# Up products of three feed-forward blocks read shifted activations, their second tile a copy

## What is computed

```
def conv_ffn(h, w_in, dw, w_out):          # layers 0 and 1
    u = causal_dwconv(h @ w_in, dw)        # [512,1024] @ [1024,5632]
    gate, val = u[..., :D_FF], u[..., D_FF:]
    return (jax.nn.silu(gate) * val) @ w_out    # [512,2816] @ [2816,1024]
...
    x = x + conv_ffn(rmsnorm(x, norm_ffn_g[layer]), ffn_w_in[layer], ffn_dw[layer], ffn_w_out[layer])
...
    a, val = jnp.split(rmsnorm_2(x, norm_ffn_g) @ w_up, 2, axis=-1)     # layer 2
    a = causal_dwconv_2(a, conv_w, conv_b)
    return x + (jax.nn.gelu(a) * val) @ w_down
```

## Time and profile before

| | us |
|---|---|
| median of 3 runs | 2596.2 (2595.59 to 2596.39) |
| the profiled execution, its own time | 2603.86 |
| its span | 2602.1 |
| TensorE busy in it | 2510.2 (96%) |
| DVE, ACT, POOL busy | 1336.2, 1123.0, 995.2 |
| mean granted clock | 0.985 |

### The profile page before, as it was taken

One profiled execution on the slowest core, in us unless ns is written; L12 is line 12 of the kernel. 1 busy time (PEld: TensorE's weight loads), 2 busy tenths in 40 slices (PEclk: granted clock), 3 DMA queues, 4 the chain that ended last, 5 costly groups with the idle time before them and its releaser, 6 DMA issues.

```text
span 2602.1 us, 62231 instructions
## 1 busy us (share of the span) xinstructions
PE 2510.2 (96%) x25266; PEld 2370.8 (91%) x25266; DVE 1336.2 (51%) x2034; ACT 1123.0 (43%) x1653; POOL 995.2 (38%) x488
## 2 busy tenths in 40 slices
PE   7999898999999999998999999999999999999998
PEld 6888886997999999977989999999998769999998
DVE  7666564513477741798523677622153344455521
ACT  8844445544433432425534344433245444444422
POOL 3333220562344444325423444444443104444442
PEclk9899999999999999999999999999999999999999
DMA  4221001351223233323222332233222103223232
GB/s 153 76 67 50 1 1 63 99 177 41 90 97 97 97 98 107 121 65 113 82 65 65 97 97 91 96 106 120 83 95 68 47 1 97 97 89 97 96 99 74
DMA packets 62180, 219.43 MB, mean 84 GB/s; under 512 B 6752, under 2 KB 9184, under 8 KB 61408
## 3 DMA queue, kind: packets, MB, share of 16 engines
q1 hardware_dynamic: 58880, 207.76, 24.8%
q10 hardware_dynamic: 3168, 9.75, 1.0%
HBM read 213.29 MB, written 4.19 MB: 84 GB/s over the span
## 4 chain that ended last, share of the span: by engine, by line
PE 83%; DVE 8%; issue 6%; ACT 2%; POOL 1%; DMA 0%; DVEq 0%; POOLq 0%; ACTq 0%
PE psum L571 70%; DVE psum L2698 5%; PE psum L713 3%; PE psum L721 2%; PE psum L1072 1%; PE psum L1021 1%; PE psum L1251 1%; PE psum L1290 1%; POOL wl L520 1%; DVE psum L2269 1%; ACT wh L1382 0%; PE psum L1253 0%; PE psum L683 0%; PE psum L1060 0%; PE psum L1278 0%
## 5 line engine op out<-in xcount | busy, mean ns | idle before, releaser
L520 POOL TENSOR_TENSOR wl<-raw,wh 128x1024 fp32r<-128x1024 f32 x388 | 949.1, 2455 | 1461.8 <-ACT wh L1382 1461.7
L571 PE MATMUL psum<-acth,wh 128*128 128x256 f32 x3792 | 763.4, 283 | 18.3 <-DVE actl L2789 8.0
L571 PE MATMUL psum<-actl,wh 128*128 128x256 f32 x3792 | 752.8, 280 | 0.0
L571 PE MATMUL psum<-acth,wl 128*128 128x256 f32 x3792 | 752.4, 280 | 0.0
L1382 ACT ACTIVATE wh<-raw 128x1024 fp32r<-128x1024 f32 x388 | 407.1, 1056 | 624.0 <-PE psum L571 600.5
L571 PEld LDWEIGHTS psum<-acth,wh 128*128 128x128 f32 x3792 | 582.4, 189 | 35.8 <-issue 28.1
L571 PEld LDWEIGHTS psum<-actl,wh 128*128 128x128 f32 x3792 | 581.6, 189 | 0.0
L571 PEld LDWEIGHTS psum<-acth,wl 128*128 128x128 f32 x3792 | 581.1, 189 | 0.0
L2628 DVE TENSOR_TENSOR cu<-psum,rstd 128x512 f32<-128x512 f32 x132 | 91.0, 690 | 237.8 <-PE psum L571 220.6
L571 PE MATMUL psum<-hidh,wh 128*128 128x256 f32 x1056 | 209.5, 276 | 0.0
L571 PE MATMUL psum<-hidl,wh 128*128 128x256 f32 x1056 | 209.3, 276 | 0.0
(11 more groups left out here) (443 smaller groups left out, 4056.0 us busy)
## 6 DMA issues: line engine op xcount, KB each, us to landing
raw<-in_weights SPq DMA_DIRECT2D x388, 512.0 KB, 3.4
xt<-in_x SPq DMA_DIRECT2D x4, 512.0 KB, 5.5
xt<-in_x ACTq DMA_DIRECT2D x1, 2048.0 KB, 9.3
out_x<-xt SPq DMA_DIRECT2D x6, 256.0 KB, 2.3
mem<-in_mem ACTq DMA_DIRECT2D x1, 1024.0 KB, 11.1
memn<-memh ACTq DMA_DIRECT2D x1, 1024.0 KB, 5.6
memn<-meml ACTq DMA_DIRECT2D x1, 1024.0 KB, 9.1
memh<-memn ACTq DMA_DIRECT2D x1, 1024.0 KB, 4.7
```

The costliest lines, as they stand in the source:

```text
L520: pool.tensor_tensor(wl[:, s, :], raw[:, s, :], wh[:, s, :].bitcast(F32), ALU.subtract).then_inc(split_done, 1)
L571: ins = pe.matmul(out[:, n:n + HALF], w, m[:, n:n + HALF], start=first and n == 0, stop=last and n + HALF >= out.shape[1])
```

## The change

The activations of the three up stages go to new tensors `uph` and `upl`, 160 bytes above acth and actl and over the same memory, so at 192. The second tile of each up stage (tile 1) reads `firsth` and `firstl` instead, at zone + 49,184 and 16,384 above that, which is 224 beyond a multiple of 512. They are filled during `xo0`, `xo1` and `out2`: for each block ACT copies uph to firsth after its square, and DVE copies upl to firstl after its addition to rstd. Two semaphores count the copies, and tile 1 waits for 8 of each. Tile 1 is taken out of the loop, which now begins with tile 2; two tiles follow it instead of three. To make room, 256 bytes are added behind actl, `eps` moves into the tail of `par`, and `omu` moves to the end of the memory; `tmp`, `sq`, `rstd` and `zone` stay where they were. The other stages that read acth and actl are as before.

```diff
         acth = place("acth", [P, KT, T], F32R)
         actl = place("actl", [P, KT, T], F32R)
-        par = place("par", [P, NPAR])
+        cursor[0] += 256
+        uph, upl = (at("up" + n, [P, KT, T], F32R, act_at + 160 + 16384 * j) for j, n in enumerate("hl"))
+        par = place("par", [P, NPAR + 6])
+        eps = par[:, NPAR:NPAR + 6]
         common = place("common", [P, 3 * P])
-        omu = place("omu", [P, 7 * KT])
-        eps = place("eps", [P, 6])
+        omu = at("omu", [P, 7 * KT], F32, 229120)
...
         cu = place("cu", [P, 4, T + 2])
+        firsth, firstl = (at("first" + n, [P, KT, T], F32R, zone + 49184 + 16384 * j) for j, n in enumerate("hl"))
...
             def ffn(l):
                 up, norm = f"up{l}", f"norm_ffn{l}"
-                tile(up, 0, norm, acth, actl)
+                tile(up, 0, norm, uph, upl)
                 norm_total(norm)
-                dense(up, norm, acth, actl, units=2 * FT - 4, skip=1)
-                for j in range(2 * FT - 3, 2 * FT):
-                    tile(up, j, norm, acth, actl)
+                pe.wait_ge(first_hi, KT * (l + 1))
+                pe.wait_ge(first_lo, KT * (l + 1))
+                tile(up, 1, norm, firsth, firstl)
+                dense(up, norm, uph, upl, units=2 * FT - 4, skip=2)
+                for j in range(2 * FT - 2, 2 * FT):
+                    tile(up, j, norm, uph, upl)
...
+                        if again:
+                            act.wait_ge(hi_ready, i * 4 + (g0 + s + 1))
+                            hold()
+                            act.activation(again[:, i * 4 + s, :], h[:, i * 4 + s, :].bitcast(F32),
+                                           ACT.Identity).then_inc(first_hi, 1)
...
-                deltas_normed(f"xo{l}", 1, f"norm_ffn{l}")
+                deltas_normed(f"xo{l}", 1, f"norm_ffn{l}", h=uph, again=firsth)
...
+                        if again:
+                            dve.wait_ge(lo_ready, i * 4 + (g0 + s + 1 + SC))
+                            dve.tensor_copy(again[:, k, :], l[:, k, :].bitcast(F32)).then_inc(first_lo, 1)
```

More of the change, by code:

```diff
@@ L344, in build_program @@
         cu = place("cu", [P, 4, T + 2])
+        firsth, firstl = (at("first" + n, [P, KT, T], F32R, zone + 49184 + 16384 * j) for j, n in enumerate("hl"))
+        assert act_at % 512 == 32 and zone % 512 == 192
         cg, cv, sg = (place("ffn_" + n, [P, 2, T]) for n in ("cg", "cv", "sg"))
@@ L375, in build_program @@
         fmax, fneg, fsum, frec = (place("fox_" + n, [P, 8, 4]) for n in ("max", "neg", "sum", "rec"))
-        assert cursor[0] <= nc.sbuf_usable_end
+        assert cursor[0] <= 229120
         over = zone + 8192
@@ L428, in build_program @@
         mid_split = sem("mid_split")
+        first_hi, first_lo = sem("first_hi"), sem("first_lo")
         x_ready = sem("x_ready")
@@ L501, in _ @@
             sp.dma_start(common[:, :], dram["c_common"]).then_inc(common_in, 16)
-            sp.dma_start(par[:, :], dram["par"]).then_inc(par_in, 16)
+            sp.dma_start(par[:, 0:NPAR], dram["par"]).then_inc(par_in, 16)
             with sp.Fori(0, UNITS // SLOTS) as i:
@@ L1462, in deltas, with deltas_normed @@
                         weight_high(UNIT0[stage] + skip + s + SLOTS, i)
-            def deltas_normed(stage, per, norm, gain=None, h=acth):
+            def deltas_normed(stage, per, norm, gain=None, h=acth, again=None):
                 x0, sq0 = plan(stage, "x"), plan(norm, "sq")
@@ L2130, in hybrid @@
                         sigmoids(2 * k + 6, 2 * k + 8)
-                deltas_normed("out2", 1, "norm_ffn2")
+                deltas_normed("out2", 1, "norm_ffn2", h=uph, again=firsth)
             def last_norm():
@@ L2196, in residual, with residual_normed @@
                         added(stage, 1, skip, i, s)
-            def residual_normed(stage, per, norm, gain, acc, col=0, h=acth, l=actl, bias=None):
+            def residual_normed(stage, per, norm, gain, acc, col=0, h=acth, l=actl, bias=None, again=None):
                 x0, sq0, g0, n = plan(stage, "x"), plan(norm, "sq"), plan(norm, "split"), len(acc)
@@ L2611, in attention @@
                 head_lows(3)
-                residual_normed(f"xo{l}", 1, f"norm_ffn{l}", ["norm_ffn_g"], [rstd], l * KT)
+                residual_normed(f"xo{l}", 1, f"norm_ffn{l}", ["norm_ffn_g"], [rstd], l * KT, uph, upl, again=firstl)
             def ffn(l):
@@ L2964, in hybrid @@
                     lows("branch", yh, yl, i)
-                residual_normed("out2", 1, "norm_ffn2", ["norm_ffn_g_2"], [rstd])
+                residual_normed("out2", 1, "norm_ffn2", ["norm_ffn_g_2"], [rstd], 0, uph, upl, again=firstl)
             def ffn2(scaled):
```

## The result

| | before | after |
|---|---|---|
| median | 2595.89 us (4 runs, 2593.49 to 2596.39) | 2617.85 us (4 runs, 2613.95 to 2624.54) |
| ratio | | 1.0083, 95% interval 1.0067 to 1.0098 |
| span of the profiled execution | 2602.1 us | 2612.2 us |

The forecast was 2576.0 us. The time is that of the rival in which all three stages fail, 2617.3 us; that the two agree to 0.6 us is luck in part, since the four runs spread over 10.6 us.

What follows compares the result with a forecast made beforehand. TensorE, busy 96% of the span, was taken to bound the kernel through the distance between matmul starts. Terms -20.2 (tiles 2 to 43), +0.1 and -0.2 (tile 0) gave -20.2 us, rounded: 2596.2 to 2576.0 us, range 2572.5 to 2591.

Steps and rivals of the forecast that it cites:

- the rival in which all three stages fail: Up stages behind tile 1, and down stages after: slow speed in all three, 2617.3 us; two or three failing had 12%.
- Tiles 2 to 43 move from 32 to 192: Up stages, 2016 matmuls each: 3.34 ns less per matmul in the fast speed, 6.73 us a stage, 20.2 us for three.
- the prediction's four: Starts of down0, down1, down2 and out2 at 192, right behind a run at 32 without a break; all four fast.
- 3.34 ns a matmul in the fast case: Up stages, tiles 2 to 43: 116.64 - 113.30 ns gained per matmul, 6.73 us a stage.
- the 1767 that the prediction named: Sign of the fast speed: about 1767 matmuls in a 200 us stretch of each up stage, where 1717 stood.
- 1.15 ns and 4.49 ns in the slow case: Loss per matmul: up stages 117.79 - 116.64 ns, 2.3 us a stage; down product 113.30 to 117.79 ns, 4.7 us.
- That the down stage takes over the up stage's speed: Down product at 192 follows without a break; behind a slow up stage its 1056 matmuls go at 117.79 ns, 4.7 us.
- What was costed at nothing: Copies on ACT and DVE, two added waits (at most 0.8 us) and the loop's later start: all taken as 0.
- The rival on the other side: Two or three up stages fail, tile 1 at 224 passing on a slow speed: 2603.6 or 2617.3 us; 12%.
- That up2 might come out differently from up0 and up1: Rival of one failing stage: up2 follows a fast tile 0, the other two a slow one; 2589.8 us, 11%.
- the 7.7 us between the profiled execution and the median: Profiled execution of 2603.86 us lay 7.7 us above the runs' median; no reason known, difference carried over to the median.
- The rule of two read ports: TensorE's matmuls: independent SBUF read ports, so weight loading steals no bandwidth; placement would not matter and the sum would be 0.

## Why the prediction was wrong

**The step that failed** stands under "Tiles 2 to 43 move from 32 to 192": "I take the fast speed, because tile 1 is at 224, and 224 and 32 are both odd multiples of 32 bytes while 192 is an even one." The prediction called this the step that it leaned on, and gave 68% to all three stages being fast. Three things in it were wrong. 224 doesn't have the 116.7 ns of 32 but 118.3. Odd and even multiples of 32 bytes are no classes: the distances are alike in places 256 bytes apart, and among the odd places they range from 116.7 to 120 ns. And whether an exit leads to the fast speed is no property of the place that is left, but of the point in its cycle at which it is left: after the change's 48 matmuls that was position 8 or 1 of the cycle at 224, both slow, and after 42 it was 2 or 3, both fast. The evidence that I had counted was sound for what it showed. In the trace before the up stages at 32 repeat 116 117 120 113, and the six exits from runs in this cycle into 192 without a break, the prediction's four among them, fall on all four of its points and are all fast. But that is this cycle at 32. It said nothing of 224, and behind a tile 0 at 192 tile 1 at 32 doesn't even come into this cycle, but into the one of 2, which has a slow exit.

**The terms of the sum were right.** 3.34 ns a matmul in the fast case: with the copy at 32 the stretches hold the 1767 that the prediction named, and the kernel came out 22.8 us under before by the ratio (15.8 to 29.6) where the sum was -20.2. 1.15 ns and 4.49 ns in the slow case: 2617.3 us, measured 2617.85. That the down stage takes over the up stage's speed was right in every profile with up products at 192.

**What was costed at nothing cost nothing that the runs can tell from zero:** the copies, the two waits and the moved loop, at 0.9993 (0.9977 to 1.0009) of before with the up products and the copy at 32. DVE's copy was 0.42 us and not 0.49 to 0.69.

**The rival on the other side** named the mechanism and its price, with 12%, and gave as one of its causes that "224 isn't like 32 at all". Its chance was set too low: the one place on which everything rested had no row in the trace, and a coin toss behind it would have been the honest chance. That up2 might come out differently from up0 and up1 did not happen. The prediction was right to watch tile 0's speed, but wrong to tie it to the stage: in the profile after, up1's tile 0 was fast like up2's, because xo1 had come out fast.

**The spread.** The prediction took the 7.7 us between the profiled execution and the median as unexplained; the two profiles show differences of that size between executions: 6.8 us up to the gate product, 1.3 and 1.7 us for kv0 and xo1.

**The rule of two read ports**, weighed in the prediction from the Trainium skill (TensorE: Matmul & The Clock Gate, "Step-by-step: what each phase is for"), would, as the prediction read it, have given no change. The runs speak against that reading: placement alone moved a matmul of one shape at one clock between 113.3 and 120.0 ns. Whether it is the weights' reads that the activations meet, no run shows; what makes the cycles stays open, since no run varied the place of the weights.

## What to carry to other kernels

Where TensorE bounds a kernel that loads weights for every matmul, measure the distance between starts for the place of the moving operand early; a few bytes of address were worth 3% to 6% of it here, and a run without breaks at one place kept the speed it began with. To steer into the better speed, look at the repeating distances and durations of the run ahead and at the point where it is left, and don't judge by the place alone. One good entry is no evidence of the next: what came before the lead-in shifted the point by one. Choose a length whose exits are good for each way of coming in, and measure it over several executions.

## What was not expected

- Eight remainders modulo 256 gave in long runs, per matmul of 256 columns: 113.3 or 117.8 ns (192), 116.7 (32), 117.3 (160), 117.8 (64), 118.3 (224), 118.7 (128), 120.0 (96 and 256). All but 192 and 32 have one long run each, so a second speed of theirs isn't excluded, and 160 has one: 118.6 ns in the 48 matmuls of tile 1.
- Within 1 or 2 ns the distances repeat: after 4 matmuls in the long up stages at 32 (116 117 120 113), after 8 at 224, after 6 at 96 (115 124 118 121 117 125). At 113.3 ns they are constant.
- The kernel with everything at 192 spread over 27.6 us in 10 runs, the one before over 17.5 us in 25 runs on the same chip, and the change over 10.6 us in 4. The counts differ, so these say little more than that the undecided one spreads most.
